# Eighteen extra matmuls on constants ahead of two semaphore waits of TensorE in a two-layer flow-matching backbone

## The chip, the cores and the metric

The kernel runs on one core of a Trainium2 chip as one launch. The metric is the device time of that core in microseconds. Three executions of the kernel before took 1110.96, 1112.47 and 1115.43 us, a median of 1112.47 us. Everything is computed in float32.

## The reference, cut to what matters

One inference step goes through two layers, for 128 context tokens and 128 latent tokens. Layer 0 is the even one (HGRN2 beside attention), layer 1 the odd one (retention). Each layer ends in a mixture of 32 experts, of which a token uses two.

```python
for l in range(DEPTH):                                   # DEPTH = 2
    mc, ms = ada_mod(c_ctx[None], mod_w[l], mod_b[l]), ada_mod(c, mod_w[l], mod_b[l])
    hc = modulate(rms_norm(xc, norm1_g[l]), mc[0], mc[1])
    hs = modulate(rms_norm(xs, norm1_g[l]), ms[0], ms[1])
    ...                                                  # even_mixer (l = 0) or odd_mixer (l = 1), residual
    hc = modulate(rms_norm(xc, norm2_g[l]), mc[3], mc[4])
    hs = modulate(rms_norm(xs, norm2_g[l]), ms[3], ms[4])
    xc = xc + mc[5] * hier_moe(hc, *moe_args)
    xs = xs + ms[5] * hier_moe(hs, *moe_args)

def hier_moe(h, w_group, b_group, w_expert, b_expert, w_gate, w_up, w_down):
    g_prob = softmax(x @ w_group + b_group)              # 4 groups
    p_grp, g_idx = top_k(g_prob, 1)
    e_logit = (x @ w_expert + b_expert)[group g_idx]     # 8 experts in the group
    e_w, e_idx = top_k(softmax(e_logit), 2)
    combine = one_hot(8 * g_idx + e_idx) * e_w / sum(e_w) * p_grp
    act = silu(x @ w_gate) * (x @ w_up) * combine        # for every expert
    return act @ w_down
```

## The kernel before, in words

The work of each engine is written out by hand in program order; engines meet only at semaphores, so an instruction of TensorE that waits holds all that stands behind it. All matrix products go through the helper `matmul` (line 643) and the transposes of the token streams through `turn_stream` (line 681). In float32 a `matmul` call leaves two records in the trace, so six calls are twelve records.

Weights come through a ring of six slots of 2 MB (`load` and the loop at lines 496 to 516, on SyncE's queue). A slot is loaded again once TensorE has counted up `used` for it. The order of the stream is fixed, but for the mixture the number of the expert is read from `ORDER`, which VectorE writes late in the routing.

The mixture of a layer is `moe(l)` on each engine. Ahead of it `project_out` ends with two transposes and two sets of `logits` (the router's 36 columns). TensorE then stands at `pe.wait_ge(mask_ready, l + 1)` (line 938) while VectorE picks the group and the two experts of each token (lines 1819 to 1872) and counts up `mask_ready` at line 1872. Behind the wait stand the prefix sums over the mask (five matmuls of 32 columns, lines 939 to 943), `start_zero(0)` (two matmuls of one row by 512 columns that clear the output banks), and the first `gather` (sixteen matmuls of 128 columns that sort tokens by expert; it waits for the selection matrices that VectorE builds from the prefix sums, lines 1892 to 1921). Then come ten steps (`step(i)`) over the experts' weights: gate, up and down products and a `scatter` each.

At the border of the layers TensorE runs `moe(0)`, a rest of it behind a branch (line 1051, for tokens that did not fit), `logit_shift(1, 4)` (eighteen thin matmuls of 36 columns, sixteen on the router's weights and two on biases, lines 685 to 695), then the wait `pe.wait_ge(xhat_ready, 3)` at line 1080 for ScalarE's normalised stream 0 (line 1223), `turn_stream(0, normed)`, two tiles of `odd_part(0, 0, ...)`, `turn_stream(1, normed)`, and all of the input projection of layer 1 in matmuls of 512 columns. ScalarE and VectorE copy each turned stream to `HT` (lines 1213 and 1562) before TensorE can use it.

`keep_warm(k, bank)` (lines 673 to 676) is there already: k matmuls of the identity by 512 columns of the constants into a bank that nobody reads. The kernel before calls it twice inside layer 0, as `keep_warm(5, 5)` at line 795. It waits for nothing and nothing waits for it.

Of the kernel before, what the change touches and what calls it, by code (L numbers as in the profile page):

```python
# [120 lines left out]
def backbone(nc, A, O, MROW):  # L121
    ctx = ExitStack()
    with ctx:
# [28 lines left out]
        def cst(name):  # L152
            a, b = CONST_AT[name]
            return const[:, a:b]
# [257 lines left out]
        def bcast(ap, shape):  # L412
            return ap.broadcast_to(shape)
# [20 lines left out]
        def _(sp):  # L434
            def source(item):
                kind = item[0]
                if kind == "mod":
                    _, l, b, q = item
                    v = A["mod_w"][l].rearrange("(p k) n -> p k n", k=KT)
                    return v[:, 4 * q:4 * q + 4, D * b:D * b + D]  # L440
                if kind == "even_in":
                    v = A["even_w_in"][0].rearrange("(k p) n -> p k n", k=KT)
                    return v[:, :, 512 * item[1]:512 * item[1] + 512]
                if kind == "odd_in":
                    v = A["odd_w_in"][0].rearrange("(k p) n -> p k n", k=KT)
                    return v[:, :, 512 * item[1]:512 * item[1] + 512]
                if kind == "state":
                    return A["state_ret"][0, 0, item[1]].rearrange("h (j p) v -> p (h j) v", p=P)
                w = A["even_w_out"] if kind == "even_out" else A["odd_w_out"]
                return w[0].rearrange("(k p) n -> p k n", p=P)[:, 4 * item[1]:4 * item[1] + 4, :]  # L450
# [190 lines left out]
        def _(pe):  # L641
            def matmul(out, lhsT, rhs, start, stop, **kw):
                return nc.tensor.matmul(out, lhsT, rhs, start=start, stop=stop, skip_group_check=True, **kw)  # L643
# [29 lines left out]
            def keep_warm(k, bank):  # L673

                for _ in range(k):
                    matmul(PS[:, bank, :], ident, const[:, 0:BANK], True, True)

            def turn_stream(s, x):

                for k in range(KT):  # L680
                    mm = nc.tensor.transpose(PS[:, 2 * s + k // 4, P * (k % 4):P * (k % 4) + P],  # L681
                                             x[:, s, P * k:P * k + P], ident)
                mm.then_inc(ht_done, 1)

            def logit_shift(l, bank):

                pe.wait_ge(router_in, 32 * (l + 1))
                pe.wait_ge(late_params_in, 16 * 12)
                pe.wait_ge(cols_ready, 4 * l + 4)
                for s in range(S):  # L690
                    at = PS[:, bank, 64 * s:64 * s + NG + NE]
                    for k in range(KT):
                        matmul(at, bcast(COLS[:, l, COL_OF[3], s, k:k + 1], [P, P]), RW[:, k, :], k == 0, False)
                    mm = matmul(at, cst("ones")[0:1, :], rbias[:, l, :], False, True)
                mm.then_inc(lshift_done, 1)
# [234 lines left out]
            def moe(l):  # L930
                ov = OV[l]

                def start_zero(a):

                    for half in range(2):
                        matmul(PS[:, 2 * a + half, :], zero, const[0:1, 0:BANK], True, False)

                pe.wait_ge(mask_ready, l + 1)
                matmul(PS[:, 5, 0:NE], cst("upper"), MASK[:, 0, :], True, True)
                matmul(PS[:, 5, 64:64 + NE], cst("ones"), MASK[:, 0, :], True, False)  # L940
# [135 lines left out]
                matmul(PS[:, 3, 0:SUB], zero, const[0:1, 0:SUB], False, True).then_inc(branch_done, 1)  # L1076

            moe(0)
            logit_shift(1, 4)
            pe.wait_ge(xhat_ready, 3)  # L1080
            turn_stream(0, normed)

# [104 lines left out]
            pe.wait_ge(ret_state_ready, 16)  # L1187
            project_out("odd_out", 4, MIXC, 2)
            moe(1)


        @block.scalar
        def _(act):
# [167 lines left out]
            def moe(l):  # L1361
# [12 lines left out]
                def step(i):  # L1374
                    _, lap, js, _ = STEPS[i]
                    t, par, last = NSTEP * l + i, i % 2, i == NSTEP - 1
                    act.wait_ge(used, AT[("moe", l, lap, js[1][-1])] + 1)
                    A_(SILB, PS[:, 6, 0:FE], SILU).then_inc(silu_ready, 1)  # L1378
                    if not last:
                        act.wait_ge(gather0_done, t + 2)  # L1380
                        xg_half(0, 1 - par).then_inc(xg0_ready, 1)
                    act.wait_ge(turn_done, t + l + 2)
                    A_(ACTT[:, :, :].rearrange("p j t -> p (j t)"), PS[:, 7, 0:256], COPY).then_inc(actt_ready, 1)
                    if not last:
                        wselt(1 - par).then_inc(wselt_ready, 1)
                    act.wait_ge(used, AT[("moe", l, lap, js[2][-1])] + 1)
                    A_(YG[:, 1, :], PS[:, 5, :], COPY).then_inc(yg1_ready, 1)  # L1387
# [117 lines left out]
        def _(dve):  # L1505
# [5 lines left out]
            def mod_rows(l, b, n, bank):  # L1511

                dve.wait_ge(used, AT[("mod", l, b, 1)] + 1)
                if n != 2:
                    read_columns(n - 1, bank, 0)
                if n >= MODBUF:
                    stored = sum(x in ROW_BLOCKS for _, x in MODS[:n - MODBUF + 1])
                    if stored:
                        dve.wait_ge(rows_out, 32 * stored)
                val = modval[:, n % MODBUF, :]  # L1520
                ins = V.tensor_tensor(val, PS[:, bank, 0:QUART], modbias[:, b, :], ALU.add)
                if b in (1, 4):
                    st.link(ins)
                    ins = V.scalar_tensor_tensor(out=val, in0=val, scalar=1.0, in1=gainrow[:, b // 4, :],
                                                 op0=ALU.add, op1=ALU.mult)
                ins.then_inc(mod_ready, 1)
# [704 lines left out]
```

## Time and profile before

| | us |
|---|---|
| median of three executions | 1112.47 |
| the profiled execution's own time | 1112.32 |
| its span, first to last instruction | 1110.5 |
| TensorE busy | 948.6 (85% of the span) |
| VectorE busy | 277.5 (25%) |
| ScalarE busy | 195.9 (18%) |
| granted TensorE clock, mean | 0.931 of full |
| DMA | 329.20 MB, mean 296 GB/s |

Times in the trace are microseconds from the start of the span. PE is TensorE's matmul side, DVE is VectorE, ACT is ScalarE; L643 is line 643 of the kernel. A line of the timeline is a start, a duration, an engine, a source line, an operation with what it writes and reads, a count of records, and in brackets how long the engine had been idle and who released it. A row of the windows view is a stretch and its length, then for PE, weight load, DVE, ACT and POOL the busy time and the count, then the granted TensorE clock (1.00 is 2.4 GHz, 0.50 is 1.2 GHz), the share of the DMA engines, and GB/s.

### The profile page before, as it was taken

How to read it: one execution, taken by the hardware profiler on the slowest of the kernel's cores; microseconds unless marked ns; L12 is line 12 of the kernel's file. 1: busy time of each engine (PE TensorE's matmuls, PEld its weight loads, DVE VectorE, ACT ScalarE, POOL GpSimd, SP SyncE). 2: the span in 40 equal slices, each digit the busy share in tenths (PEclk: the TensorE clock that was granted, in tenths of full speed). 3: DMA queues.
4: the chain of work that ended last, by engine and by line, in shares of the span. 5: the costliest groups of instructions: out<-in, count | busy, mean ns of one | idle time of the engine just before them, and what ended most of it. 6: DMA issues, size and time to landing. Idle time of an engine off the chain costs nothing.

```text
span 1110.5 us, 14254 instructions
## 1 busy us (share of the span) xinstructions
PE 948.6 (85%) x6023; PEld 534.6 (48%) x6023; DVE 277.5 (25%) x703; ACT 195.9 (18%) x361; POOL 52.4 (5%) x78
## 2 busy tenths in 40 slices
PE   2799999989599997766699999999996999977753
PEld 1585555574465554433444444444445655544421
DVE  1110235641642121100212212232026421211002
ACT  2211121250211010000222122344001110100001
POOL 3000000120200000000000010000002000000000
PEclk8799999989699998888789999999996999989986
DMA  9999729994369999999954445034832799999991
GB/s 298 401 361 361 304 86 381 410 409 172 114 280 378 419 416 416 416 415 417 388 205 151 152 151 189 38 123 190 335 149 111 274 383 419 417 416 417 416 416 64
DMA packets 80312, 329.20 MB, mean 296 GB/s; under 512 B 5724, under 2 KB 6100, under 8 KB 63604
## 3 DMA queue, kind: packets, MB, share of 16 engines
q1 hardware_dynamic: 74820, 311.71, 71.1%
q0 software_dynamic: 5360, 16.49, 4.2%
q8 instruction: 50, 0.82, 0.3%
q14 instruction: 18, 0.15, 0.0%
q10 hardware_dynamic: 64, 0.03, 0.0%
HBM read 322.12 MB, written 6.09 MB: 296 GB/s over the span
## 4 chain that ended last, share of the span: by engine, by line
PE 70%; DMA 18%; DVE 4%; SPq 4%; issue 2%; ACT 1%; DVEq 0%; ACTq 0%
PE PS L643 68%; DMA ring<-in_moe_w_down 16%; DMA ring<-in_even_w_in 2%; SPq L514 2%; SPq L457 1%; PE PS L681 1%; DVE scratch L1829 0%; DVE H L1577 0%; SPq L495 0%; PE PS L1143 0%; PE PS L956 0%; PE PS L961 0%; SPq L489 0%; DVE X L1572 0%; PE PS L776 0%
## 5 line engine op out<-in xcount | busy, mean ns | idle before, releaser
L643 PE MATMUL PS<-ring,scratch 128*32 128x256 f32 (+4 forms) x2720 | 311.1, 473 | 79.9 <-DMA ring<-in_moe_w_gate 44.7
L643 PEld LDWEIGHTS PS<-ring,scratch 128*32 128x32 f32 (+2 forms) x2720 | 147.4, 130 | 240.8 <-issue 201.2
L643 PE MATMUL PS<-ring,HT 128*128 128x512 f32 x576 | 253.5, 596 | 2.5 <-ACT HT L1213 1.7
L643 PEld LDWEIGHTS PS<-ring,HT 128*128 128x128 f32 x576 | 108.7, 191 | 133.4 <-issue 129.2
L643 PE MATMUL PS<-scratch 128*128 128x512 f32 (+2 forms) x440 | 117.3, 438 | 4.4 <-issue 1.5
L643 PEld LDWEIGHTS PS<-scratch 128*128 128x128 f32 (+1 forms) x440 | 56.2, 193 | 58.4 <-issue 54.3
L643 PE MATMUL PS<-scratch,H 128*128 128x128 f32 x640 | 83.5, 287 | 0.0
L643 PEld LDWEIGHTS PS<-scratch,H 128*128 128x128 f32 x640 | 78.2, 200 | 10.2 <-issue 10.2
L1977 DVE TENSOR_TENSOR scratch<-PS,scratch 128x256 f32<-128x256 f32 x20 | 8.5, 424 | 280.4 <-ACT scratch L1378 280.4
L643 PE MATMUL PS<-ring,cpad 128*32 128x256 f32 x768 | 48.3, 406 | 14.7 <-DMA ring<-in_mod_w 14.7
L1378 ACT ACTIVATE scratch<-PS 128x256 f32<-128x256 f32 x20 | 7.7, 384 | 269.5 <-PE PS L643 269.5
L643 PE MATMUL PS<-HT,ring 128*128 128x256 f32 x192 | 44.1, 393 | 5.3 <-DMA ring<-in_even_w_in 5.3
L643 PEld LDWEIGHTS PS<-HT,ring 128*128 128x128 f32 x192 | 37.8, 198 | 11.2 <-issue 5.7
L643 PEld LDWEIGHTS PS<-ring,cpad 128*32 128x32 f32 x768 | 24.8, 116 | 33.2 <-issue 13.6
L1387 ACT ACTIVATE scratch<-PS 128x512 f32<-128x512 f32 x20 | 11.9, 597 | 123.2 <-PE PS L643 123.2
L1568 DVE TENSOR_TENSOR scratch<-PS,scratch 128x1024 f32<-128x1024 f32 x8 | 9.8, 1223 | 88.1 <-PE PS L643 88.1
L1971 DVE COPY scratch<-PS 128x512 f32<-128x512 f32 x20 | 13.8, 692 | 69.6 <-PE PS L643 69.6
L1206 ACT ACTIVATE scratch<-X 128x1024 f32<-128x1024 f32 x10 | 10.6, 1055 | 100.0 <-DVE X L1572 88.2
L1984 DVE COPY scratch<-PS 128x512 f32<-128x512 f32 x20 | 13.7, 686 | 35.2 <-PE PS L643 35.2
L643 PE MATMUL PS<-const 128*128 128x512 f32 (+2 forms) x40 | 21.2, 666 | 0.9 <-issue 0.9
L1369 ACT ACTIVATE scratch<-PS 128x512 f32<-128x512 f32 x20 | 11.9, 597 | 48.5 <-PE PS L643 48.5
L643 PE MATMUL PS<-scratch,const 128*128 128x32 f32 x20 | 4.7, 403 | 17.5 <-DVE small L1872 17.5
(280 smaller groups left out, 648.8 us busy)
## 6 DMA issues: line engine op xcount, KB each, us to landing
ring<-in_moe_w_gate SPq DMA_DIRECT2D x64, 1024.0 KB, 17.0
ring<-in_moe_w_up SPq DMA_DIRECT2D x64, 1024.0 KB, 17.4
ring<-in_moe_w_down SPq DMA_DIRECT2D x64, 1024.0 KB, 17.2
ring<-in_mod_w SPq DMA_DIRECT2D x24, 2048.0 KB, 15.5
ring<-in_odd_w_in SPq DMA_DIRECT2D x12, 2048.0 KB, 13.6
ring<-in_even_w_in SPq DMA_DIRECT2D x7, 2048.0 KB, 16.1
ring<-in_odd_w_out SPq DMA_DIRECT2D x4, 2048.0 KB, 7.8
scratch<-mod_rows POOLq DMA_DIRECT2D x12, 512.0 KB, 7.5
```

What stands on the lines that cost most here:

```text
L457: sp.dma_start(dst, src).then_inc(landed[n % RING], 16)
L514: sp.dma_start(dst.rearrange("p (a b) -> p a b", b=src.shape[2]), src)\
L643: return nc.tensor.matmul(out, lhsT, rhs, start=start, stop=stop, skip_group_check=True, **kw)
L681: mm = nc.tensor.transpose(PS[:, 2 * s + k // 4, P * (k % 4):P * (k % 4) + P], x[:, s, P * k:P * k + P], ident)
L1206: A_(junk, X[:, s, :], SQUARE, accum_out=sumsq[:, s:s + 1]).then_inc(sq_ready, 1)
L1369: return A_(XG[:, par, 4 * half:4 * half + 4, :].rearrange("p k t -> p (k t)"), PS[:, 4 + half, :], COPY)
L1378: A_(SILB, PS[:, 6, 0:FE], SILU).then_inc(silu_ready, 1)
L1387: A_(YG[:, 1, :], PS[:, 5, :], COPY).then_inc(yg1_ready, 1)
L1568: st.link(V.tensor_tensor(GATE[:, s, :], PS[:, 2 * s:2 * s + 2, :].rearrange("p b n -> p (b n)"), GATE[:, s, :], ALU.mult))
L1971: return V.tensor_copy(XG[:, par, 4 * half:4 * half + 4, :].rearrange("p k t -> p (k t)"), PS[:, 4 + half, :])
L1977: V.tensor_tensor(ACTB, PS[:, 6, FE:2 * FE], SILB, ALU.mult).then_inc(act_ready, 1)
L1984: V.tensor_copy(YG[:, 0, :], PS[:, 4, :]).then_inc(yg0_ready, 1)
```

## The change

`keep_warm(6, 6)` is called at two more places of TensorE's program: in `moe(l)` just ahead of the wait for the mask, so once in each layer, and once between `logit_shift(1, 4)` and the wait for `xhat_ready` at the border of the layers. That makes 18 more matmul calls, 36 records, all into bank 6. No wait, semaphore, transfer or other instruction is altered; no other engine's program changes.

```diff
@@ -935,6 +935,7 @@
                     for half in range(2):
                         matmul(PS[:, 2 * a + half, :], zero, const[0:1, 0:BANK], True, False)
 
+                keep_warm(6, 6)
                 pe.wait_ge(mask_ready, l + 1)
                 matmul(PS[:, 5, 0:NE], cst("upper"), MASK[:, 0, :], True, True)
                 matmul(PS[:, 5, 64:64 + NE], cst("ones"), MASK[:, 0, :], True, False)
@@ -1077,6 +1078,7 @@
 
             moe(0)
             logit_shift(1, 4)
+            keep_warm(6, 6)
             pe.wait_ge(xhat_ready, 3)
             turn_stream(0, normed)
 
```

TensorE's program at the mask of layer 0, before: the row on `RWG,HT` is the router's logits, the one of 128x32 the prefix sums over the mask, the one on `const` the clearing of two banks, the one on `scratch,H` the first gather.

```order
84 L681 MATMUL PS<-const,X 128x128 x8
85 L643 MATMUL PS<-RWG,HT 128x36 x8
86 L643 MATMUL PS<-scratch,const 128x32 x5
87 L643 MATMUL PS<-const 128x512 x2
88 L643 MATMUL PS<-scratch,H 128x128 x16
```

The same place now:

```order
84 L681 MATMUL PS<-const,X 128x128 x8
85 L643 MATMUL PS<-RWG,HT 128x36 x8
86 L643 MATMUL PS<-const 128x512 x6
87 L643 MATMUL PS<-scratch,const 128x32 x5
88 L643 MATMUL PS<-const 128x512 x2
89 L643 MATMUL PS<-scratch,H 128x128 x16
```

Six matmuls stand between the logits and the first instruction that waits for the mask; the order of the rest is as it was. Next, TensorE's program at the border of the layers, before: `RW,COLS` and `rbias` are `logit_shift(1, 4)`, the rows of L681 `turn_stream`, `ring,HT` the projection into layer 1.

```order
192 L643 MATMUL PS<-RW,COLS 128x36 x8
193 L643 MATMUL PS<-rbias,const 128x36
194 L643 MATMUL PS<-RW,COLS 128x36 x8
195 L643 MATMUL PS<-rbias,const 128x36
196 L681 MATMUL PS<-const,scratch 128x128 x8
197 L643 MATMUL PS<-ring,HT 128x512 x2
```

And now:

```order
193 L643 MATMUL PS<-RW,COLS 128x36 x8
194 L643 MATMUL PS<-rbias,const 128x36
195 L643 MATMUL PS<-RW,COLS 128x36 x8
196 L643 MATMUL PS<-rbias,const 128x36
197 L643 MATMUL PS<-const 128x512 x6
198 L681 MATMUL PS<-const,scratch 128x128 x8
199 L643 MATMUL PS<-ring,HT 128x512 x2
```

Here the six stand between the last bias matmul and the first transpose, which is the instruction that waits for `xhat_ready`.

## Rows read from the trace of the kernel before

**Rows 1.** The page's chain that ended last, by line.

```profile
PE PS L643 68%; DMA ring<-in_moe_w_down 16%; DMA ring<-in_even_w_in 2%; SPq L514 2%; SPq L457 1%; PE PS L681 1%; DVE scratch L1829 0%; DVE H L1577 0%; SPq L495 0%; PE PS L1143 0%; PE PS L956 0%; PE PS L961 0%; SPq L489 0%; DVE X L1572 0%; PE PS L776 0%
```

**Rows 2.** Timeline of TensorE at the mask of layer 0.

```profile
280.11 1.07 PE L681 MATMUL PS<-const,X 128*128 128x128 f32 x8
281.97 1.98 PE L643 MATMUL PS<-RWG,HT 128*128 128x36 f32 x16 [0.78 <-DVE HT L1592]
292.95 2.34 PE L643 MATMUL PS<-scratch,const 128*128 128x32 f32 x10 [9.01 <-DVE small L1872]
295.22 3.78 PE L643 MATMUL PS<-const 1*128 1x512 f32 x4
298.93 5.24 PE L643 MATMUL PS<-scratch,H 128*128 128x128 f32 x32
```

**Rows 3.** Timeline of TensorE at the mask of layer 1.

```profile
836.40 2.39 PE L643 MATMUL PS<-RWG,HT 128*128 128x36 f32 x16 [0.78 <-DVE HT L1592]
847.25 2.34 PE L643 MATMUL PS<-scratch,const 128*128 128x32 f32 x10 [8.47 <-DVE small L1872]
...
853.23 6.23 PE L643 MATMUL PS<-scratch,H 128*128 128x128 f32 x32
```

**Rows 4.** Timeline of TensorE at the border of the layers.

```profile
552.47 1.97 PE L681 MATMUL PS<-const,scratch 128*128 128x128 f32 x8
556.10 3.78 PE L643 MATMUL PS<-ring,HT 128*128 128x512 f32 x4 [1.66 <-ACT HT L1213]
559.68 1.84 PE L681 MATMUL PS<-const,scratch 128*128 128x128 f32 x8
561.36 22.91 PE L643 MATMUL PS<-ring,HT 128*128 128x512 f32 x53
```

**Rows 5.** Timeline of ScalarE at the border: the normalised stream 0.

```profile
547.29 1.15 ACT L1223 ACTIVATE scratch<-X,small 128x1024 f32<-128x1024 f32 x1 [0.30 <-DVE small L1555]
```

**Rows 6.** Timeline of VectorE: the first selection matrices of layer 0.

```profile
297.96 0.61 DVE L1921 SCALAR_TENSOR_TENSOR scratch<-const,scratch 128x128 f32<-128x128 f32 x2
```

**Rows 7.** Windows: the mask of layer 0, and of layer 1 (last row).

```profile
284.90:292.90 8.00, 0.00 (x0) 0.00 (x0) 7.28 (x32) 0.41 (x2) 2.85 (x1) 0.50 0.19 76
...
298.90:301.80 2.90, 2.90 (x14) 2.87 (x14) 0.20 (x1) 0.00 (x0) 0.00 (x0) 0.50 0.00 0
...
853.30:858.20 4.90, 4.90 (x23) 4.90 (x24) 0.10 (x1) 0.60 (x1) 0.00 (x0) 0.50 0.00 0
```

**Rows 8.** Windows: the border of the layers.

```profile
552.50:561.30 8.80, 7.14 (x21) 4.56 (x21) 1.37 (x4) 2.54 (x5) 0.00 (x0) 0.50 1.02 375
561.40:570.00 8.60, 8.60 (x22) 3.82 (x22) 2.24 (x7) 4.49 (x8) 0.56 (x1) 1.00 0.41 154
```

**Rows 9.** Windows: waits for weights and the work behind them, mixture of layer 0.

```profile
419.80:424.70 4.90, 4.90 (x48) 2.66 (x52) 0.00 (x0) 0.00 (x0) 0.00 (x0) 0.50 1.02 425
...
443.70:448.60 4.90, 0.00 (x0) 0.00 (x0) 0.00 (x0) 0.55 (x1) 0.00 (x0) 1.00 1.02 421
448.70:449.80 1.10, 0.00 (x0) 0.00 (x0) 0.00 (x0) 0.00 (x0) 0.00 (x0) 0.50 1.02 425
...
473.80:475.90 2.10, 0.00 (x0) 0.00 (x0) 0.00 (x0) 0.52 (x1) 0.00 (x0) 1.00 1.01 421
...
480.00:482.70 2.70, 2.70 (x28) 1.48 (x32) 0.00 (x0) 0.00 (x0) 0.00 (x0) 0.50 1.01 422
```

**Rows 10.** Timeline of TensorE: the same kinds of matmul elsewhere, at full clock.

```profile
186.64 4.46 PE L643 MATMUL PS<-const 128*128 128x512 f32 x10
...
308.61 1.98 PE L643 MATMUL PS<-const 1*128 1x512 f32 x4
...
314.12 2.05 PE L643 MATMUL PS<-scratch,H 128*128 128x128 f32 x16
```

**Rows 11.** Windows: DMA while the mixture of layer 0 begins.

```profile
340.00:345.00 5.00, 5.00 (x71) 2.52 (x68) 0.28 (x1) 0.60 (x1) 0.00 (x0) 1.00 0.69 232
345.00:350.00 5.00, 5.00 (x51) 2.35 (x53) 0.00 (x0) 0.00 (x0) 0.00 (x0) 1.00 1.02 422
```

## The prediction

> **What bounds the kernel now.** I read the chain of waits first: 68% of it is TensorE's matmuls and 16% the experts' down weights [rows 1]. So the kernel alternates between TensorE and DMA, and the question at each of the three edited places is which of the two counts there. Next I read TensorE's timeline at the three places, then the windows view for the granted clock.
>
> At the mask of layer 0 the logits end at 281.97 + 1.98 = 283.95, and TensorE stands for 9.01 us until VectorE's mask at 292.95 [rows 2]. In layer 1 the logits end at 838.79 and the wait of 8.47 us ends at 847.25 [rows 3]. Both waits are VectorE's; TensorE is not late there. The clock is at half (1.2 GHz) from 284.9, and is at half still when the gather runs [rows 7].
>
> At the border it is the other way round. ScalarE finished the normalised stream 0 at 547.29 + 1.15 = 548.44 [rows 5]. TensorE came to it only at 552.47, with no idle time in brackets [rows 4]. There is no wait at that place: TensorE is 4.0 us late by itself. The clock there is at half until 561.3, at full from 561.4, and TensorE is busy from then on [rows 8].
>
> Do losses and gains at these places reach the end? At the border yes: TensorE works through and the DMA share behind it is 0.41 [rows 8]. At the masks also, though the later steps of the mixture wait for DMA. DMA is at a share of 0.69 at 340 to 345 and at 1.02 only from 345 [rows 11]: until then transfers wait for slots that TensorE empties, and the saturated stretch starts earlier or later with TensorE. VectorE's ranking, which gives the experts' numbers, follows the same prefix sums and gather, so it moves with them.
>
> **What the six matmuls cost by themselves.** Ten such records took 4.46 us at full clock, 0.43 each with the tail of the last one off [rows 10]. At half clock a record of 512 columns takes 0.86 (four in 3.78 with a tail; [rows 2, 4]). So twelve take 5.1 us at full clock, 10.3 at half, and 5.1 + c/2 if the first c us are at half. How soon does the clock rise once dense work starts? Rows show dense work still at half clock for 2.7 us (480.0), 2.9 (298.9), 4.9 (419.8), 4.9 (853.3) and, at the border itself, from 556.10 to 561.3, 5.2 us [rows 4, 7, 8, 9]. Three of five lie near 5, and the border's own is 5.2, which I take.
>
> **The border.** Added: 5.1 + 5.2/2 = 7.7 us at 552.47, all on the path, as no wait covers it. Saved: what follows now runs at full clock. The transposes of stream 0 take 1.07 [rows 2] and not 1.97 (0.9 less). The copy to HT (1.66 idle) stays. The four projection records go from 3.58 (556.10 to 559.68) to 4 x 0.43 = 1.72 (1.9 less). The transposes of stream 1 go from 1.68 (559.68 to 561.36) to 0.9 (0.8 less). From 561.36 the clock was full anyway. Saved 3.6, net +4.1. Bounds: a rise 2.7 us into the six gives 6.45 - 3.6 = +2.9; six at full clock from the start give 5.1 - 3.6 = +1.5; no rise at all gives +10.3. The second transpose needs ScalarE's stream 1, made after its copy of stream 0; the 1.66 and 1.72 us ahead of it cover its 1.2 us.
>
> **The mask of layer 0.** The six start at 283.95 and end at 289.1 at full clock and at 291.7 with c = 5.2; both lie ahead of 292.95, so they delay nothing. What can they give? Only work behind 292.95 that the clock is still high for. Idle TensorE kept a full clock for 2.1 us at 473.8 and for 4.9 at 443.7, and then fell, while idle [rows 9]. From 289.1 that is 291.2 to 294.0, so the prefix matmuls from 292.95 find the clock already down or for one microsecond. If it drops early inside the six as it did at 284.9, they end later and the clock lasts longer. At full clock the ten prefix records would take 1.2 us and not 2.27 (sixteen logit records with the same weight load took 1.98, [rows 2]): 1.07 at most. It passes on, since VectorE builds the selection from the sums. I take 0.4, between 0 and 1.07.
>
> **The mask of layer 1.** Here the logits themselves slow down (2.39 against 1.98, [rows 2, 3]), so the clock is at half when the six start at 838.79. They take 5.1 + 1.4 to 2.6, end at 845.3 to 846.5, ahead of 847.25, and the clock then stays up until 847.4 to 851.4 (2.1 to 4.9 more). The prefix matmuls mostly profit: 0.8 of the 1.07.
>
> The gather is not reached in either layer. Between the six and the gather (298.93, 853.23) lie some 7 to 10 us with nothing but thin or one-row matmuls, and no row shows a full clock held over an idle stretch longer than 4.9. That one-row matmuls don't help is in the rows too: start_zero streamed from 295.22 to 298.93 and the clock stayed at half until the gather had run 2.9 us [rows 2, 7].
>
> Of TensorE: Matmul & The Clock Gate (section Terms), the Trainium skill says that the penalty is the throttled time times (1 - K/N), here half of it. The stretch at half clock round the mask of layer 0 is 284.9 to 301.8, 16.9 us [rows 7]; with as much at layer 1 and 8.8 us at the border [rows 8] it is 42.6, and as an estimate by that rule 21.3 us could be won and the time would be 1091.0. The rows disagree: in 284.9 to 292.9 TensorE has no record at all [rows 7], and an engine that stands pays nothing for its clock.
>
> **Sum.** +4.1 - 0.4 - 0.8 = +2.9 on the profiled execution's own 1112.3: 1115.2 us. The median shown is 1112.47, 0.15 above that execution, which changes nothing.
>
> **Rivals.**
> 1. The clock is held up to the gather. Then each layer saves 1.07 on the prefix sums; 0.36 since start_zero takes 1.98 [rows 10] and the gather goes when its selection is there (297.96 + 0.61 = 298.57, [rows 6]) and not at 298.93; and on the gather itself 5.08 less 3.8 (two times 1.89, [rows 10]) = 1.3 in layer 0, some 2.3 in layer 1. That is 2.7 + 3.7 = 6.4, with the border +4.1: 1110.0; with a quick rise at the border 1108.8, and 1107.4 with no half clock there at all. For it: VectorE's selection may let a late fall meet an early gather. Against: the 7 to 10 us above.
> 2. Slower: matmuls on constants don't raise the clock. Point of decision: do six identity matmuls count as work or as little as start_zero did, whose stream of 3.7 us raised nothing? Then the border costs 10.3 in full (what follows rises as before), layer 0 ends at 283.95 + 0.9 + 10 x 0.86 = 293.5, 0.5 late, and layer 1 at 838.8 + 10.3 = 849.1, 1.8 late: +12.6, 1124.9. For it: start_zero. Against: start_zero uses one row of the array, the six use all 128; in the stretch at 186.64 the clock was full throughout, though it was so before.
> 3. Half the time at half clock comes back at all three places, (16.9 + 16.9 + 8.8)/2 = 21.3: 1091.0. As a mechanism of this kernel it asks that the waits for VectorE shorten with TensorE's clock, which no row hints at.
> 4. The change does what its words say and the border has a wait: if TensorE reached line 1080 by 548.4, 4 us of the six were covered and the border came to +0.1, giving 1111. Against: even at full clock the second half of logit_shift alone is 2 us and starts at 548.35.
>
> On rival 2 the Trainium skill has a rule in TensorE: Matmul & The Clock Gate (Part 4): transposes do not count as busy for the clock in the same way, and the six have a transpose's stationary operand. By it alone the result would be rival 2's 1124.9. The trace speaks against the rule: the clock rose at 561.3 behind 1.6 us of nothing but transposes [rows 4, 8].
>
> **How the numbers follow.** Forecast 0.76 (1111.4 to 1118 on its own), rival 1 0.10, rival 2 0.09, rival 3 0.01, rival 4 0.04. A measurement of this kernel tells a change of about 0.5% (5.6 us) from none. Faster by more: rival 3, and 0.05 of rival 1, whose lowest case of 1107.4 lies within the spread of executions of that bound, 0.06. Slower by more: rival 2, and 0.10 for the forecast's upper end (+4.3 at the border, nothing at the masks, executions that spread by 4.5 us), 0.19. The rest, 0.75, is no change. The range runs from rival 1's 1109.4 to 1119; it leaves out rivals 2 and 3 and little else.
>
> **What the changed profile would show.** At the border six matmuls of 7 to 8 us from about 552, straight behind logit_shift, a clock that rises inside them, and the long run of projection records beginning some 13 us after the end of logit_shift, not 8.9 (552.47 to 561.36). At the masks the wait for VectorE shrinks to about 4 us (layer 0) and 1 us (layer 1), the prefix matmuls take between 1.2 and 2.3 us, and the gather starts at half clock. I am wrong if the gather runs in 3.8 us, if a wait on ScalarE shows in front of the transposes, or if the six take 10 us.

## The result: 4 us slower, and where they went

Twenty executions of the changed kernel have a median of 1117.64 us (1113.89 to 1122.67), twenty of the kernel before 1113.01 us (1110.24 to 1119.38). The ratio is 1.0038, with a 95% interval of 1.0025 to 1.0052: 4.2 us slower, 2.8 to 5.8. The forecast was +2.9 us; a change of up to 5.6 us either way counted there as none. The profiled execution after took 1113.89 us (span 1112.0). That is the fastest of its twenty, so its own distance to the 1112.32 before (1.6 us) says little; stretches are compared instead.

TensorE at the branch and the border before, up to where [rows 4] begin (the four lines are the last scatter, the one-row matmul that releases VectorE for the residual, and the start of `logit_shift`):

```profile
538.96 3.67 PE L643 MATMUL PS<-scratch 128*128 128x512 f32 x8 [0.76 <-issue]
542.56 0.40 PE L643 MATMUL PS<-const 1*128 1x32 f32 x2
542.89 0.41 PE L643 MATMUL PS<-RW,COLS 128*128 128x36 f32 x2
546.07 1.78 PE L643 MATMUL PS<-RW,COLS 128*128 128x36 f32 x14 [2.76 <-issue]
```

The same place and the border after, columns as there:

```profile
537.32 3.67 PE L643 MATMUL PS<-scratch 128*128 128x512 f32 x8 [0.76 <-issue]
544.59 0.40 PE L643 MATMUL PS<-const 1*128 1x32 f32 x2 [3.60 <-issue]
544.92 2.51 PE L643 MATMUL PS<-RW,COLS 128*128 128x36 f32 x16
...
551.49 0.64 PE L643 MATMUL PS<-rbias,const 1*128 1x36 f32 x2
552.06 7.57 PE L643 MATMUL PS<-const 128*128 128x512 f32 x12
559.46 1.04 PE L681 MATMUL PS<-const,scratch 128*128 128x128 f32 x8
562.16 1.98 PE L643 MATMUL PS<-ring,HT 128*128 128x512 f32 x4 [1.66 <-ACT HT L1215]
563.98 1.04 PE L681 MATMUL PS<-const,scratch 128*128 128x128 f32 x8
564.85 19.48 PE L643 MATMUL PS<-ring,HT 128*128 128x512 f32 x45
```

The six stand straight behind `logit_shift`, with no idle time on either side, and take 7.40 us to the next instruction (forecast 7.7). From the end of `logit_shift` to the long projection it is 12.79 us (552.06 to 564.85), before it was 8.89. That is +3.9 (forecast +4.1). The windows show the clock rising inside the six, after some 4.3 us:

```profile
552.10:556.30 4.20, 4.20 (x6) 1.80 (x6) 0.01 (x1) 0.00 (x0) 0.00 (x0) 0.50 1.05 387
556.50:559.40 2.90, 2.90 (x8) 1.24 (x7) 0.00 (x0) 0.00 (x0) 0.00 (x0) 1.00 0.96 355
```

At the masks, against [rows 2, 3] (layer 0 first, then layer 1):

```profile
280.93 3.63 PE L643 MATMUL PS<-RWG,HT 128*128 128x36 f32 x16 [0.78 <-DVE HT L1594]
284.37 8.28 PE L643 MATMUL PS<-const 128*128 128x512 f32 x12
292.48 1.20 PE L643 MATMUL PS<-scratch,const 128*128 128x32 f32 x10
293.61 1.98 PE L643 MATMUL PS<-const 1*128 1x512 f32 x4
297.11 5.39 PE L643 MATMUL PS<-scratch,H 128*128 128x128 f32 x32 [1.52 <-DVE scratch L1923]
...
839.90 1.98 PE L643 MATMUL PS<-RWG,HT 128*128 128x36 f32 x16 [0.79 <-DVE HT L1594]
841.71 5.40 PE L643 MATMUL PS<-const 128*128 128x512 f32 x12
850.80 2.34 PE L643 MATMUL PS<-scratch,const 128*128 128x32 f32 x10 [3.70 <-DVE small L1874]
853.07 3.78 PE L643 MATMUL PS<-const 1*128 1x512 f32 x4
856.78 5.46 PE L643 MATMUL PS<-scratch,H 128*128 128x128 f32 x32
```

The two layers have changed places against the forecast. In layer 0 the clock was already at half for the logits; the six took 8.28 us and TensorE reached the prefix sums late. VectorE had finished the mask before:

```profile
291.68 0.15 DVE L1874 COPY small<-small 128x1 f32<-128x1 f32 x1
```

That is 291.83 against 292.48, 0.65 us late. In return the prefix sums ran in 1.20 us and start_zero in 1.98, so that TensorE then waits 1.52 us for the selection. In layer 1 the clock was full for logits and six (5.40 us), it fell while TensorE waited 3.70 us, and the prefix sums took their old 2.34. The gather ran at half clock at its start, as forecast. The clock had differed before any added matmul: up to the logits of layer 0 both kernels run the same program, and these took 1.98 us before and 3.63 after. Windows of layer 0: the six at half and at full clock, the prefix sums with start_zero, and the gather's first half:

```profile
284.40:290.10 5.70, 5.70 (x8) 2.46 (x9) 4.97 (x21) 0.21 (x1) 2.80 (x1) 0.50 0.17 70
290.30:292.40 2.10, 2.10 (x6) 0.95 (x5) 1.86 (x16) 0.20 (x1) 0.00 (x0) 1.00 0.00 0
292.50:296.90 4.40, 3.08 (x15) 1.73 (x13) 3.30 (x19) 0.00 (x0) 0.00 (x0) 1.00 0.00 0
297.10:300.30 3.20, 3.19 (x15) 3.20 (x16) 0.38 (x2) 0.00 (x0) 0.00 (x0) 0.50 0.00 0
```

### The profile page after: what moved, and what is told of

Read it like the earlier page. It is cut to its first block, busy times and chain, and to the rows that moved or that the text cites. A ratio compares the mean times of both kernels' runs of the same rounds, so it can differ in the third digit from the quotient of the medians.

```text
span 1112.0 us, 14326 instructions
## 1 busy us (share of the span) xinstructions
PE 965.8 (87%) x6059; PEld 542.0 (49%) x6059; DVE 277.2 (25%) x703; ACT 195.8 (18%) x361; POOL 52.2 (5%) x78
## 4 chain that ended last, share of the span: by engine, by line
PE 71%; DMA 19%; SPq 4%; DVE 4%; issue 2%; ACT 1%; DVEq 0%; ACTq 0%
PE PS L643 68%; DMA ring<-in_moe_w_down 16%; DMA ring<-in_even_w_in 2%; SPq L514 2%; SPq L457 1%; PE PS L681 0%; PE PS L1145 0%; SPq L491 0%; PE PS L957 0%; PE PS L962 0%; DVE scratch L1831 0%; SPq L489 0%; DVE X L1574 0%; PE PS L776 0%; ACT scratch L1208 0%
## 5 line engine op out<-in xcount | busy, mean ns | idle before, releaser
L643 PE MATMUL PS<-const 128*128 128x512 f32 (+2 forms) x76 | 40.7, 681 | 3.6 <-issue 3.6
L1208 ACT ACTIVATE scratch<-X 128x1024 f32<-128x1024 f32 x10 | 10.6, 1055 | 103.0 <-DVE X L1574 90.9
L643 PEld LDWEIGHTS PS<-const 128*128 128x128 f32 (+1 forms) x76 | 16.1, 222 | 23.3 <-issue 22.6
```

The costliest lines, as they stand in the source:

```text
L1208: A_(junk, X[:, s, :], SQUARE, accum_out=sumsq[:, s:s + 1]).then_inc(sq_ready, 1)
```

## The experiments

All figures in us are the ratio and its interval times 1113. Each kernel ran twelve times (`border_twelve` and `border_thin` six times) beside the kernel before. "Border stretch" is from the last scatter of layer 0 to the long projection (22.40 before, 27.53 after); "mask stretch" is from the second set of logits to the first gate matmul (layer 0: 23.03 before, 22.39 after). Stretches are from one profiled execution of each kernel, times from all of its executions.

**The parts apart.** `border_only`:

```diff
             logit_shift(1, 4)
+            keep_warm(6, 6)
             pe.wait_ge(xhat_ready, 3)
```

> Only the six matmuls at the border, none at the masks. Theory: 7 to 8 us on the path less 3.6 us for what runs at full clock behind them, +4.1 us (ratio 1.0037). Rival (the border is free, or its matmuls raise nothing): 0 or +10.3 us. In the trace: the six end with the clock at full, the transposes behind them in about 1.0 us.

Measured: +3.5 (1.7 to 5.2). Border stretch 26.70, the six in 7.07. From the end of `logit_shift` to the long projection it is 12.46 us, 3.6 more than before.

`masks_only`:

```diff
+                keep_warm(6, 6)
                 pe.wait_ge(mask_ready, l + 1)
```

> Only the six matmuls ahead of the wait for the mask, in both layers, none at the border. Theory: -0.4 and -0.8 us, -1.2 us (ratio 0.9989), the gather still at half clock in its first part. Rival (the clock is held up to the gather): -6.4 us. Rival (they run late and delay the prefix sums): +1 to +2 us.

Measured: -0.6 (-2.2 to +1.1). Mask stretches 23.17 and 22.74. In the nine kernels without matmuls at the mask of layer 0 (the one before among them) that stretch was 23.0 to 24.5, mean 23.4; in the eight without any at layer 1 it was 23.0 to 23.9, mean 23.6. In the two with six it averages 22.8 and 23.0. That makes some 1.2 for both together, in the direction of the forecast but no larger than the scatter of such stretches, and the interval of the times holds zero: the gain is likely, not shown. The waits for VectorE came out as forecast here (3.81 us in layer 0, 0.34 in layer 1), and the prefix sums took 2.35 and 1.30. The two parts (+3.5, -0.6) add up to +2.9, inside the interval of the whole. The rival of a clock held to the gather is out for six matmuls, and so, by nearly all of the interval, is a loss of 1 to 2 us.

**Is the border on the path?** `border_twelve` has `keep_warm(12, 6)` there.

> Twelve matmuls at the border, none at the masks. Theory: the second six run at full clock and are all on the path, so this is 5.1 us slower than the run with six, +9.2 us on the kernel before. Rival (TensorE waits at the border anyway, or is early later): less than 3 us between the two.

Measured: +9.9 (7.1 to 12.6). Border stretch 31.99, 5.3 more than with six. By the times the two kernels are 6.4 us apart. The second six cost about their full duration of 5.1, if not more: nothing hides matmuls at that place.

**Do matmuls of one row raise the clock?** `border_thin`:

```diff
+            for _ in range(6):
+                matmul(PS[:, 6, :], zero, const[0:1, 0:BANK], True, True)
```

> Six matmuls of one row by 512 columns (as start_zero has) at the border instead of six full ones. If one-row matmuls do not raise the clock: they take 10.3 us at half clock, nothing behind them gets faster, +10.3 us. If they raise it as full ones do: +4.1 us as with the full ones.

Measured: +8.6 (6.1 to 11.0); border stretch 32.72, +10.3. That this is the forecast to the tenth is luck: the six took 10.5 us, the first half of `logit_shift` ended 0.9 later in this execution, and what stands behind the six was 1.0 faster. Windows of this kernel: the thin ones themselves, then what follows, then the projection.

```profile
553.00:563.40 10.40, 10.40 (x13) 3.77 (x13) 0.00 (x0) 0.00 (x0) 0.00 (x0) 0.50 0.92 340
563.50:570.20 6.70, 5.04 (x13) 2.96 (x13) 1.37 (x4) 2.54 (x5) 0.00 (x0) 0.50 0.02 6
570.40:575.00 4.60, 4.60 (x18) 2.57 (x17) 2.24 (x7) 3.36 (x7) 0.56 (x1) 1.00 0.09 23
```

PE is busy for 10.4 us without a gap and the clock stays at 0.50; it rises only at 570.3, behind the transposes and 3.2 us of full matmuls. So 10.4 us of busy time were not enough here. Two things set these matmuls apart from the six, and no run parts them: they use one row of the array and not 128, and their stationary row, the one that clears banks, holds nothing but zeros. The prediction's rival 2 was a true description of these matmuls and not of the six: with the identity and all 128 rows, constants do raise the clock.

**Places with a wait.** `behind_turn` has `keep_warm(2, 6)` behind `turn_stream(0, normed)`, `before_branch` has `keep_warm(3, 6)` behind the last scatter of layer 0; neither has other additions.

> Two full matmuls behind the transposes of stream 0, where TensorE really waits (1.66 us for the copy to HT), no others. Theory: at half clock they take 3.4 us, 1.8 over the wait, and the clock rises up to 1.7 us sooner: +0.5 to +1.5 us. Rival (a real wait makes extra matmuls free and the clock gains): -1 us.

Measured: +0.1 (-1.6 to +1.9). The two took 2.23 us in place of the wait of 1.66, the border stretch was 21.38. By the stretch a gain of 1.0, by the times none that can be told.

> No extra matmuls at the masks or behind logit_shift; three full ones (2.6 us at full clock) behind the last scatter of layer 0, ahead of the branch at whose far side TensorE stood idle for 2.8 to 3.6 us. Theory: they run inside that gap, VectorE has 4 us in hand there, the clock stays up for more of logit_shift (3.6 to 2.0 us for its second half) and of what follows (up to 3.6 us): -1 to -4 us. Rival (the gap begins only when TensorE has finished, so they are on the path): +2.6 us less what the clock gives, 0 to +2 us.

Measured: -1.2 (-3.2 to +0.8). Timeline of TensorE:

```profile
547.14 2.74 PE L643 MATMUL PS<-const 128*128 128x512 f32 x6
550.86 0.40 PE L643 MATMUL PS<-const 1*128 1x32 f32 x2 [0.99 <-issue]
551.20 1.97 PE L643 MATMUL PS<-RW,COLS 128*128 128x36 f32 x16
553.10 0.41 PE L643 MATMUL PS<-rbias,const 1*128 1x36 f32 x2
553.44 1.97 PE L643 MATMUL PS<-RW,COLS 128*128 128x36 f32 x16
555.34 0.63 PE L643 MATMUL PS<-rbias,const 1*128 1x36 f32 x2
556.80 1.97 PE L681 MATMUL PS<-const,scratch 128*128 128x128 f32 x8 [0.82 <-ACT scratch L1225]
```

They fill the idle time at the branch (0.99 left) and both halves of `logit_shift` run in 1.97. But the one-row matmul that releases VectorE for the residual comes 7.2 us after the scatter's start and not 3.6 (550.86 against 542.56, where the scatters began at 543.63 and 538.96), and now the normalised stream 0 is late: TensorE waits 0.82 us and the clock has fallen when it goes on. The stretch is 22.02, 0.4 less. Most of the gain was turned into a new wait.

**TensorE late or waiting at the border?** `shift_later` puts all of `logit_shift` behind the transposes, `split_shift` only its second half:

```diff
-            logit_shift(1, 4)
+            logit_shift(1, 4, (0,))
             pe.wait_ge(xhat_ready, 3)
             turn_stream(0, normed)
+            logit_shift(1, 4, (1,))
```

> No extra matmuls: the wait for the normalised stream 0 and its transposes are put ahead of logit_shift(1, 4), which then runs while the stream is copied to HT. If TensorE is 4 us late at the border as the trace says, work is moved into waits: TensorE idles some 1 to 2.5 us for the stream and covers 1.66 us of the copy: -2 to 0 us. If the place had a wait as the change assumed, no difference.

Measured: +0.2 (-1.8 to +2.2). TensorE stood 5.53 us for stream 0, and the work put behind is longer than the wait it covers; border stretch 23.57.

> No extra matmuls: only the second half of logit_shift(1, 4) (stream 1, 3.6 us at half clock) is moved behind the wait for the normalised stream 0 and its transposes. If TensorE is late at the border and its own work is the bound there, it fills the 1.66 us in which TensorE waits for the copy to HT: -1.7 us, border stretch (last scatter to the long projection) 22.4 to about 20.7 us. If the real bound is the stream from ScalarE, nothing changes.

Measured: -3.2 (-5.5 to -1.0), faster than the kernel before without a single matmul more. Timeline of TensorE:

```profile
552.31 1.97 PE L681 MATMUL PS<-const,scratch 128*128 128x128 f32 x8
554.07 3.47 PE L643 MATMUL PS<-RW,COLS 128*128 128x36 f32 x16
557.47 0.64 PE L643 MATMUL PS<-rbias,const 1*128 1x36 f32 x2
558.04 3.67 PE L643 MATMUL PS<-ring,HT 128*128 128x512 f32 x4
561.54 1.04 PE L681 MATMUL PS<-const,scratch 128*128 128x128 f32 x8
```

The wait of 1.66 us in front of the projection records is gone; the stretch is 19.69, 2.7 less, of which 1.7 is the wait and the rest where the clock rose. With the slope of `border_twelve` this shows from both sides that the bound of the border was TensorE's own work.

**Carrying the clock to the gather, and the branch.** `masks_more` has seven matmuls ahead of the mask and two behind the prefix sums, in both layers; `masks_layer1` the same in layer 1 only:

```diff
+                if l == 1:
+                    keep_warm(7, 6)
                 pe.wait_ge(mask_ready, l + 1)
...
+                if l == 1:
+                    keep_warm(2, 6)
                 start_zero(0)
```

> Seven full matmuls ahead of the mask and two more between the prefix sums and start_zero, in both layers, none at the border. If the clock can be carried into the gather: up to -6.4 us and the first gather in 3.8 us. If it falls in between anyway: the two cost up to 1 us each layer, -1 to +2 us.

Measured: -0.8 (-2.9 to +1.3). In layer 0 the mask stretch fell to 20.64 and the gather to 3.84 us, in layer 1 only to 22.36. These two lie 4.0 under the means of the kernels without, and the border stretch is 0.7 longer (23.08). By the stretches that is a gain of 3.3; the times allow 2.9 at most.

> Seven full matmuls ahead of the mask and two behind the prefix sums in layer 1 only. The idle time of TensorE at the branch of layer 0 was 2.7 to 2.8 us in all kernels without matmuls at the mask of layer 0 and 3.5 to 3.6 us, lying ahead of the last one-row matmul, in all kernels with them. If this comes from the place of the code behind them: here 2.8 us again. If it comes from chance between executions: either value. Gain of layer 1 alone: -1 us.

Measured: -3.0 (-4.8 to -1.2), the other kernel that beats the one before. TensorE in layer 1:

```profile
841.58 3.08 PE L643 MATMUL PS<-RWG,HT 128*128 128x36 f32 x16 [0.78 <-DVE HT L1596]
844.47 8.52 PE L643 MATMUL PS<-const 128*128 128x512 f32 x14
852.83 1.20 PE L643 MATMUL PS<-scratch,const 128*128 128x32 f32 x10
853.86 3.87 PE L643 MATMUL PS<-const 128*128 128x512 f32 x8
857.66 3.84 PE L643 MATMUL PS<-scratch,H 128*128 128x128 f32 x32
...
862.33 3.67 PE L643 MATMUL PS<-ring,scratch 128*64 128x256 f32 x32 [0.61 <-issue]
```

The stretch is 20.75, against 23.6 on average without them; the gather costs 3.84, it was 6.23 [rows 3]. Yet the profiled execution was the slowest of its twelve (1114.76 us): what a stretch gives can be covered by what varies elsewhere, and -3.0 is the figure of all twelve. Part of it may come from another place, the branch of layer 1 (below).

> The split logit_shift and seven plus two full matmuls at the mask in both layers. By the sum of the stretches: -1.7 at the border, +0.7 for the longer idle time at the branch, -1.2 to -2.4 at each mask: -3 to -5 us (ratio 0.996). If the later branch takes away the time in hand for stream 0, the border gains nothing and the whole is -2 us.

Measured: -0.3 (-2.3 to +1.7), far less than the parts. Two reasons are in its trace. In layer 0 the clock fell behind the prefix sums:

```profile
283.06 7.95 PE L643 MATMUL PS<-const 128*128 128x512 f32 x14
292.28 1.30 PE L643 MATMUL PS<-scratch,const 128*128 128x32 f32 x10 [1.26 <-DVE small L1876]
293.42 6.84 PE L643 MATMUL PS<-const 128*128 128x512 f32 x8
300.18 5.79 PE L643 MATMUL PS<-scratch,H 128*128 128x128 f32 x32
```

The two behind the prefix sums and start_zero took 6.84 us, 3.87 in `masks_layer1`, and the gather 5.79: a stretch of 25.55, 2 us worse than none. In layer 1 it was 21.21. And at the border TensorE waited 1.52 us for stream 0, as the expectation feared, and the stretch there was 24.00, 4.3 more than in `split_shift`.

> Three full matmuls ahead of the mask in both layers instead of six. Theory of the clock: they end at least 6 us ahead of the mask, the clock falls again, nothing is gained at the prefix sums: 0 us at the masks. At the branch: if the idle time depends on how far the code behind is shifted, another value than 2.8 and 3.6 us may show, whole +0 to +0.7 us.

Measured: +0.7 (-1.1 to +2.6); the mask stretch of layer 0 was 24.58 and that of layer 1 23.56, no better than without.

**The idle time at the branch.** In the five kernels with matmuls at the mask of layer 0 it was 3.38 to 3.63 us (three matmuls or nine), and lay ahead of the one-row matmul that releases VectorE. In seven kernels without them it was 2.67 to 2.97, behind two further records; `masks_layer1` is one of them, as its additions run only after that branch. (`before_branch` and `shift_later` alter the place itself.) In the changed kernel VectorE is released 7.3 us after the last scatter begins and not 3.6 (544.59 - 537.32 against 542.56 - 538.96), and of the 4.0 us that stream 0 had in hand 1.6 are left. TensorE loses too: from the last scatter to the end of the first half of `logit_shift` it takes 9.4 to 10.7 us in the seven kernels (mean 10.0) and 10.6 to 11.8 in the five (mean 11.2). Of these 1.2 us some 0.6 to 0.7 are the idle time itself; the rest is a first half that runs more at half clock.

The same branch stands at the end of layer 1, with the one-row matmul behind it. Before and after:

```profile
1097.49 0.40 PE L643 MATMUL PS<-const 1*128 1x32 f32 x2 [0.86 <-issue]
1098.97 0.40 PE L643 MATMUL PS<-const 1*128 1x32 f32 x2
```

From there to the end of the span it is 13.0 us in both, so this idle time is on the path. It was 0.86 in the kernel before, 0.5 to 0.8 in five others, and none in eight, the changed kernel and `masks_layer1` among them. At the branch of layer 0 the idle time goes with what is inserted ahead of it; at that of layer 1 no such order is seen. By which mechanism (the profile calls it issue) wasn't shown, nor was it tested whether one kernel keeps its value from run to run.

## Why the prediction was right

**The border was the point, and it was read rightly.** That TensorE is late there and not waiting, and so pays for the six, is shown by `border_only`, by the slope of `border_twelve`, and from the other side by `split_shift`. The term of +4.1 measured +3.9 in the trace after, +3.6 in that of `border_only`, and +3.5 (1.7 to 5.2) by its times. Its two halves were right too: 7.4 for the six (7.7), 3.5 saved behind them (3.6).

**The masks gave about what was said, but not as was said.** Sum -1.2 by stretches, forecast -1.2, and neither is told from zero by the times. The step "both lie ahead of 292.95, so they delay nothing" failed in layer 0: it took at most 5.2 us at half clock, and the run had 5.8 (284.37 to 290.2), which made the six end 0.65 us after the mask. The step "the clock is at half when the six start" failed in layer 1, where it was full. Both lean on when the clock changes, and this differs from execution to execution (the logits of layer 0 above); only the sum of the two was fit to be forecast.

**The branch was missing.** The prediction counted no cost for instructions inserted ahead of a branch. By the means, the kernels with additions at the mask of layer 0 lose 1.2 us there, which takes back all that the masks gave. At the branch of layer 1 the changed kernel has 0.9 less than the one before. With +3.9, -1.2, +1.2 and -0.9 the stretches come to +3.0, and the times say +4.2 (2.8 to 5.8). The remaining 1.2 us are within the interval and aren't explained. So the border was foreseen, while the closeness of +2.9 for the whole is in part luck: two terms that were left out nearly cancel.

**The gather.** "Not reached" held for six in every run. It is reached with seven and two in three of the five cases (layer 0 of `masks_more`, layer 1 of `masks_layer1` and of `split_and_masks`; not in layer 1 of `masks_more` and layer 0 of `split_and_masks`). Where it works the layer's stretch falls by 2.4 to 2.8 us, so rival 1's price was right for layer 0 (2.7) and high for layer 1 (3.7).

**Smaller errors.** The prediction's range begins at "rival 1's 1109.4", but its sums for that rival are 1110.0, 1108.8 and 1107.4. The stretch at half clock at layer 1 was not as long as at layer 0: it ran from 837.9 to 858.2, 20.3 us and not 16.9, which would make rival 3 faster still. And the six do not share a transpose's stationary operand: `keep_warm` has the identity as the stationary operand, `turn_stream` as the moving one (the records `const,X` name the moving operand first, as `RWG,HT` do). The 1.6 us of transposes ahead of 561.3 had 3.6 us of full matmuls ahead of them, so they say little on what transposes do by themselves.

**The rule on throttled time** (TensorE: Matmul & The Clock Gate, Terms, in the Trainium skill) does not hold as a price here. With the six the clock's mean rose from 0.931 to 0.936 and the time rose as well, and in `masks_only`, which adds nothing to the path at the border, it rose to 0.937 while the time stayed within -2.2 to +1.1: the half-clock stretches that went were mostly ones in which TensorE waited. Nor did the page's rule on transposes reach these matmuls, whose stationary operand is the identity: they raised the clock.

## What to carry to other kernels

Before filling a wait, look whether the engine waits: a wait instruction in the source is no wait in the trace, and at the border the extra matmuls cost 7.4 us to give back 3.5. Where the engine is late and a real wait follows, move needed work into it; the same border gave 3.2 us (1.0 to 5.5) that way. `split_shift` together with `masks_layer1`, the two that were faster, was not tried. Filling a real wait gave a clear gain once (`masks_layer1`), in a trace that shows the clock carried to the next dense work; two kernels in which it was carried in one layer showed none in their times. Since the moment at which the clock changes varies from run to run, judge such a change by many executions, not by one trace.

## What the runs showed of the hardware

Matmuls that use one row of the array, a row of zeros, kept PE busy for 10.4 us without raising the clock from 1.2 GHz; identity matmuls with 128 rows, at the same place, saw it rise after 4.3 us. Whether the rows or the zeros make the difference wasn't tried. Inserting 3 to 9 matmuls a quarter of a millisecond earlier in the program moved and lengthened TensorE's idle time at a branch, from 2.7 to 3.0 us to 3.4 to 3.6.
